# Issuing the key projection between the transposes of later tiles, and loading inputs and first weights ahead of the small vectors, in a one-core encoder step

## The reference, cut to what matters

```python
def rmsnorm(x, g):
    y = xf * lax.rsqrt(jnp.mean(xf * xf, axis=-1, keepdims=True) + NORM_EPS)
    return (y * g).astype(x.dtype)
...
h = rmsnorm(x, norm_mix)
q_sb, k_sb, v_sb, q_sw, k_sw, v_sw, q_mem, gates = split_projection(h, w_in, b_gate)
...
q_sw = rmsnorm(q_sw, q_norm_sw);  k_sw = rmsnorm(k_sw, k_norm_sw)
k, v = jnp.split(rmsnorm(mem, norm_mem) @ w_mem_kv, 2, axis=-1)
```

## Time and profile before

| what | value |
|---|---|
| median of 3 runs | 4260.44 us |
| profiled execution, its time / its span | 4256.27 us / 4254.5 us |
| `project`, from the start to the first matmul of `attend` | 429.74 us |
| in it: until the first projection matmul | 45.04 us |
| start of unit 9, the first of the value block | 112.20 us |
| TensorE busy over the whole span | 83% |

### The profile page before, as it was taken

One profiled execution on the slowest core, in us unless ns is written; L12 is line 12 of the kernel. 1 busy time (PEld: TensorE's weight loads), 2 busy tenths in 40 slices (PEclk: granted clock), 3 DMA queues, 4 the chain that ended last, 5 costly groups with the idle time before them and its releaser, 6 DMA issues.

```text
span 4254.5 us, 35451 instructions
## 1 busy us (share of the span) xinstructions
PE 3514.4 (83%) x10969; PEld 1800.6 (42%) x10969; DVE 2565.3 (60%) x5586; ACT 1509.0 (35%) x3957; POOL 1749.2 (41%) x1439
## 2 busy tenths in 40 slices
PE   7999898889669988768988888996777787777777
PEld 4545665578435454423333344442332333333222
DVE  2131446611878765857866875686775776676444
ACT  2111556611453435343433435443222222233222
POOL 0000000000577677576666666666333333333332
PEclk8999889999889999879999989998999999999999
DMA  5111310044999999999999999999999999999998
GB/s 170 58 41 50 127 45 21 18 158 167 375 397 420 420 421 422 354 401 421 421 421 421 420 411 413 421 407 421 421 418 421 417 413 416 418 416 416 422 422 349
DMA packets 240318, 1402.89 MB, mean 330 GB/s; under 512 B 26096, under 2 KB 54000, under 8 KB 87280
## 3 DMA queue, kind: packets, MB, share of 16 engines
q0 software_dynamic: 165888, 1208.03, 68.8%
q1 hardware_dynamic: 74240, 192.60, 12.2%
HBM read 1368.56 MB, written 32.90 MB: 329 GB/s over the span
## 4 chain that ended last, share of the span: by engine, by line
DMA 22%; POOL 20%; PE 15%; issue 11%; DVE 9%; ACT 2%; POOLq 0%; SPq 0%; ACTq 0%; DVEq 0%
DMA ring<-in_experts_dram,idx 22%; POOL side L1276 11%; POOL ring L1265 9%; PE ps L1386 8%; DVE ring L1643 4%; PE ps L1357 2%; PE ps L1309 2%; PE ps L1334 1%; PE ps L1319 1%; ACT diag L1485 1%; DVE hot L1538 1%; DVE hot L1534 1%; DVE idx L1542 1%; DVE cand L1523 1%; ACT wgt L1476 0%
## 5 line engine op out<-in xcount | busy, mean ns | idle before, releaser
L1386 PE MATMUL ps<-ring,diag 128*128 128x512 f32 x3520 | 1769.1, 647 | 620.2 <-ACT diag L1485 611.4
L1265 POOL DMA_INDIRECT ring<-in_experts_dram,idx x1152 | 1100.6, 955 | 1991.0 <-PE ps L1386 1210.7
L1643 DVE CUSTOM_DVE_ANT_0 ring<-ring,ps 128x1024 f32<-128x1024 f32 x1152 | 1384.8, 1219 | 816.4 <-DMA ring<-in_experts_dram,idx 802.6
L1386 PEld LDWEIGHTS ps<-ring,diag 128*128 128x128 f32 x3520 | 690.6, 204 | 1607.0 <-ACT diag L1485 872.7
L1469 ACT ACTIVATE act_<-hid 128x2 f32<-128x2 f32 x576 | 117.1, 203 | 1916.0 <-DVE hid L1643 1914.8
L1276 POOL TENSOR_TENSOR side<-side,ring 128x1024 f32<-128x1024 f32 x272 | 642.6, 2362 | 57.1 <-ACT ring L1490 51.8
L1309 PE MATMUL ps<-hx,wbuf 128*128 128x256 f32 (+2 forms) x1152 | 397.1, 491 | 13.1 <-DMA hx<-hT_scratch 13.1
L1485 ACT ACTIVATE diag<-const,wgt 128x128 f32<-128x128 f32 x880 | 320.4, 396 | 19.3 <-PE ps L1386 0.5
L1490 ACT ACTIVATE ring<-ring,wgt 128x1024 f32<-128x1024 f32 x272 | 308.2, 1133 | 0.0
L1309 PEld LDWEIGHTS ps<-hx,wbuf 128*128 128x128 f32 x1152 | 223.0, 194 | 178.3 <-issue 110.0
L309 PE MATMUL ps<-w_qkv,hT 128*128 128x512 f32 (+1 forms) x720 | 285.7, 553 | 1.3 <-DVE mhT L403 1.3
(11 more groups left out here) (179 smaller groups left out, 2820.9 us busy)
## 6 DMA issues: line engine op xcount, KB each, us to landing
wbuf<-in_w_gate_o_dram SPq DMA_DIRECT2D x72, 768.0 KB, 8.4
wbuf<-in_w_q_dram SPq DMA_DIRECT2D x24, 1024.0 KB, 9.0
ring<-in_experts_dram,idx POOLq DMA_INDIRECT x1152, 17.1
wbuf<-in_w_out_dram SPq DMA_DIRECT2D x12, 1024.0 KB, 9.0
w_qkv<-in_w_in_dram SPq DMA_DIRECT2D x5, 2048.0 KB, 8.2
o_x<-o_scratch SPq DMA_DIRECT2D x9, 768.0 KB, 30.0
hT_scratch<-hT SPq DMA_DIRECT2D x9, 512.0 KB, 6.7
hx<-hT_scratch SPq DMA_DIRECT2D x9, 512.0 KB, 16.9
```

The costliest lines, as they stand in the source:

```text
L1265: i = nc.gpsimd.indirect_dma_start(out=ring[:, j % RING, :], out_offset=None, in_=A["experts"], in_offset=bass.IndirectOffsetOnAxis(ap=idx ...
L1386: last = nc.tensor.matmul(acc[:, h, :], diag[:, (by_pe(j) - 1) % 4, :], ring[:, j % RING, DM + h * HB:DM + (h + 1) * HB], start=(j % SLOTS ...
L1643: last = nc.vector.tensor_tensor_reduce(out=u, in0=u, in1=xp, scale=1.0, scalar=0.0, op0=ALU.mult, op1=ALU.add, accum_out=hid[:, j % SLOTS ...
```

## The change

Three things are done.

1. **Order on TensorE and ScalarE.** With `BEHIND = 3`, TensorE does for each tile t from 3 on the projection of keys of tile t-3 (`produce`, with `turn(u - 2)` in it) and then the transposes of tile t. Units 0 to 7 stand between transposes, unit 8 and all others behind the last tile. ScalarE evacuates unit t-4 after squaring tile t.
2. **Banks.** As banks 4 to 7 are still in use, all turns of the key block use the one bank 3, and a turn waits for all keeps before it, not for all but one. The squares of the inputs are written into the buffer `mv` rather than PSUM.
3. **Order on SyncE.** Tiles 0 and 1 are loaded right behind the constants, then the two halves of `gmix`, then the weights of the key block, then tiles 2 and 3. The second weights still follow tile 5. The four per-head gain vectors (`gq`, rows spread over 128 partitions) are loaded behind tile 10 and awaited by VectorE only at the first `kvsw` unit.

```diff
         def turn_bank(n):
-            return 3 + n % 2
+            return 3 if n < NT else 3 + n % 2
+        BEHIND = 3
...
                 sp.dma_start(xt[t % XR], TILES[t]).then_inc(x_in[t % XR], 16)
-                if t in (3, 5):
-                    load_w((t - 3) // 2)
+                if t == 1:
+                    ... gmix[:, 0, :] and gmix[:, 1, :] ... .then_inc(gmix_in, 16)
+                if t in (1, 5):
+                    load_w(t // 4)
+            o = 0
+            for name, n in (("q_norm_sw", HD), ("k_norm_sw", HD), ("q_norm_mem", MD), ("k_norm_mem", MD)):
+                sp.dma_start(gq[:, o:o + n], A[name][0:1, :].to_broadcast([P, n])).then_inc(gains_in, 16)
...
-                if n >= 2:
-                    pe.wait_ge(kept, n - 1)
+                if n >= 1:
+                    pe.wait_ge(kept, n if n < NT else n - 1)
...
+            def produce(u):
+                c, kind, t = units[u]
+                if u < NT:
+                    pe.wait_ge(h_done, u + 1)
...
+            for t in range(NX):
+                pe.wait_ge(x_nat, t + 1)
+                if t >= 2:
+                    pe.wait_ge(h_done, t - 1)
+                if t >= BEHIND:
+                    produce(t - BEHIND)
+                for c in range(KC):
+                    last = nc.tensor.transpose(ps[:, 4 + 2 * (t % 2) + c // 4, (c % 4) * P:(c % 4 + 1) * P],
+                                               xt[t % XR][:, c * P:(c + 1) * P], ident)
+                last.then_inc(x_T, 1)
+            pe.wait_ge(h_done, NX)
+            for u in range(NX - BEHIND, len(units)):
+                produce(u)
...
+            for t in range(NX):
+                act.wait_ge(x_in[t % XR], 16 * (t // XR + 1))
...
+                if t > BEHIND:
+                    evacuate(t - BEHIND - 1)
```

More of the change, by code:

```diff
@@ L101, in project @@
         gains_in = sem("gains_in")
+        gmix_in = sem("gmix_in")
         x_in = [sem(f"x_in{i}") for i in range(XR)]
@@ L184, in _ @@
             sp.dma_start(S["const"][:, :], small_dram[:, :]).then_inc(const_in, 16)
[L185 to L191, removed]
             def load_w(c):
@@ L202, in _ @@
                 sp.dma_start(xt[t % XR], TILES[t]).then_inc(x_in[t % XR], 16)
-                if t in (3, 5):
-                    load_w((t - 3) // 2)
+                if t == 1:
+                    with nc.allow_non_contiguous_dma(reason="gains, a few kilobytes"):
+                        sp.dma_start(gmix[:, 0, :], A["norm_mix"][0].rearrange("(c p) -> p c", p=P)).then_inc(gmix_in, 16)
+                        sp.dma_start(gmix[:, 1, :], A["norm_mem"][0].rearrange("(c p) -> p c", p=P)).then_inc(gmix_in, 16)
+                if t in (1, 5):
[3 more added lines that the diff above has]
+                sp.dma_start(gq[:, o:o + n], A[name][0:1, :].to_broadcast([P, n])).then_inc(gains_in, 16)
+                o += n
             for name, c in (("new_swa_k_sample", "cache_swa_k"), ("new_swa_v_sample", "cache_swa_v")):
@@ L266, in _ @@
             pe.wait_ge(const_in, 16)
[L267 to L275, removed]
             def turn(u):
@@ L291, in turn @@
                 last.then_inc(turned, 1)
-            for u, (c, kind, t) in enumerate(units):
+            def produce(u):
+                c, kind, t = units[u]
+                if u < NT:
+                    pe.wait_ge(h_done, u + 1)
                 if t == 0:
@@ L318, in _ @@
         def _(act):
[L319 to L327, removed]
             def keep(u):
@@ L346, in keep, with evacuate @@
                 i.then_inc(kept, 1)
-            for u, (c, kind, t) in enumerate(units):
+            def evacuate(u):
+                c, kind, t = units[u]
                 act.wait_ge(proj, u + 1)
@@ L377, in _ @@
                     keep(u - 2)
+            for t in range(NX):
+                act.wait_ge(x_in[t % XR], 16 * (t // XR + 1))
+                if t >= 1:
+                    act.wait_ge(x_sq, t)
+                nc.scalar.activation(S["mv"][:, :, :].rearrange("p a n -> p (a n)"), xt[t % XR], ACT.Square,
+                                     accum_out=ss[:, 0:1]).then_inc(x_sq, 1)
+                act.wait_ge(x_ms, t + 1)
+                nc.scalar.activation(ss[:, 2:3], ss[:, 1:2], ACT.Sqrt).then_inc(x_rt, 1)
+                if t > BEHIND:
+                    evacuate(t - BEHIND - 1)
+            act.wait_ge(pad_zero, 2)
+            for u in range(NX - BEHIND - 1, len(units)):
+                evacuate(u)
             keep(len(units) - 2)
@@ L382, in _ @@
         def _(dve):
-            dve.wait_ge(gains_in, 16 * 6)
             for t in range(NX + 1):
@@ L395, in _ @@
                     v = t - 1
+                    if v == 0:
+                        dve.wait_ge(gmix_in, 16 * 2)
                     dve.wait_ge(x_T, v + 1)
@@ L408, in _ @@
                 n = n_norm[u]
+                if n == 1:
+                    dve.wait_ge(gains_in, 16 * 4)
                 dve.wait_ge(squared, n)
```

## The result

The changed kernel takes 4272.15 us (median of 14 runs), the kernel before 4258.95 us in the same comparison (14 runs): a ratio of 1.0026, 95% interval 1.0014 to 1.0038. A second comparison gave 4269.93 against 4258.08 us, 1.0030 (1.0017 to 1.0044). By the medians the change costs 12 to 13 us; the intervals reach from 6 to 19 us. The forecast was 4268.2 us, 7.8 us slower, with a range of 4258 to 4275.

A forecast was written before the change was run, and what follows sets the result against it. TensorE was taken to bound the key block from 49.50 us, its head winnable. With both stalls and half clock, unit 9 moved from 112.2 to 120.0 us; that 7.8 us gave 4268.2 us, range 4258 to 4275.

The forecast's parts named there:

- Both pauses: TensorE stalls 5.3 us before turn 2 (unit 3's copy) and some 14.8 us in turn 6 (unit 7's copy).
- The rival that the early outputs pass quickly: Unit 0's output lands by X + 6, so the first stall and its half clock go: 4259.5 us; chance 0.14.
- The strict series: Tile 10, gain vectors, copies and output pass one behind another, unit 0's output landing at X + 15: 4274.4 us; chance 0.13.
- the point (X + 11.7): Landing of unit 0's output from which on the summed slowdown is over 8.5 us, the bound of no change.
- Tile 3 lands at 15.9; with 2.6 us more TensorE reaches its third iteration.: Head of the key block: the third iteration at 18.5, tile 2's transposes done by 18.2 to 19.2; 18.8 taken.
- The sum for the first stall: Unit 3's copy waits for unit 0's output behind tile 10, gains and cache copies: X + 11, bounds X + 6.0 and X + 15.
- I charge 2.2 us for half clock: TensorE loses 2.2 us at the start, bounds 0 and twice that; charged again after the first stall and at unit 9.
- The spill at 280 GB/s: Nine 512 KB DMAs ahead of unit 4's output take 16.9 us; 20.6 us from first issue to that output's landing.
- A microsecond won or lost before unit 9 reaches the end unchanged.: TensorE bounds the stage from 49.50 us on and attend follows, so the 7.8 us at unit 9 were added to the time.
- the condition I had set: The prediction is wrong if the time from unit 9 to the end differs from before by more than 3 us.
- a change within 0.2%: Whole-kernel time within 8.5 us of before, called no change; chance 0.54, against slower 0.38 and faster 0.08.
- The main case: Both stalls as summed, unit 9 7.8 us later, 4268.2 us, own range 4263 to 4272; chance 0.62.

The follow-up runs named there:

- Experiment 1: Changed kernel with the nine spill DMAs and their wait moved behind the first value output; 4250.21 us, ratio 0.9977 against the kernel before.
- experiment 2: Changed kernel with the four gain vectors and two cache copies issued behind the first value output; 4258.31 us, ratio 0.9997 against the kernel before.
- experiment 3: Changed kernel with spill, gain vectors and cache copies all issued later; 4251.14 us, ratio 0.9981 against the kernel before; again 4248.43 us, 0.9980.
- experiment 4: Kernel before with the new order of loads alone, projections still behind all transposes; 4255.75 us, ratio 0.9990 against the kernel before.
- kernel 5: Changed kernel's interleaving alone, with the loads in the order of the kernel before; 4262.61 us, ratio 1.0009 against the kernel before.

## Why the prediction came out right, and where it did not

The terms as predicted and as measured, X being the end of tile 6's transposes:

| step | predicted | measured |
|---|---|---|
| unit 0 starts | 18.8 | 20.54 |
| half clock at its start | 2.2 | 2.2 (unit 0: 20.54 to 29.61, 9.07 for 6.87) |
| X | 52.9 | 54.75 |
| unit 0's output landed, ScalarE goes on | X + 11 | X + 11.9 (66.64) |
| unit 5 starts | X + 14.8 | X + 15.6 (70.39) |
| half clock then | 2.2 | 2.4 (turn and transposes 67.78 to 70.39, 2.61 for 1.30; unit 5 to 78.36, 7.97 for 6.87) |
| last tile multiplied | X + 42.8 | X + 42.7 (97.48) |
| spill to unit 7's copy | 20.6 | 19.15 (97.48 to 116.63) |
| unit 9 starts | 117.8 | 118.67 |
| half clock then | 2.2 | 2.5 (unit 9: 118.67 to 128.09, 9.42 for 6.87) |
| attend, against before | +7.8 | +9.0 |
| time, against before | +7.8 | +13.2 and +11.9 (medians) |

**What was right.** Both pauses, their places, releasers and sizes came from two rules of this program: SyncE issues in its written order, and unit u's copy waits for unit u-3's output to land. Experiment 1 took away the second alone, experiment 2 the first alone, experiment 3 both, each with unit 9 within 2.1 us of what was expected. The rival that the early outputs pass quickly is refuted by 66.64. The strict series, X + 15, did not come either: X + 11.9 is just past the point (X + 11.7) that the prediction named.

**"Tile 3 lands at 15.9; with 2.6 us more TensorE reaches its third iteration."** This failed by 1.7 us. Of these 0.9 are the landing of tile 2, at 15.51 where 1.3 us ahead of 15.9 was expected. The rest is the way behind it. The 2.6 us is the way of a tile that finds the engines free. Here tile 2's landing at 15.51 sets the pace: its scaling (17.31), the multiplication of tile 1 that VectorE's list puts behind it (17.98), and only then tile 3's mean. That is 2.6 + 2.4 us from tile 2, where 2.4 is the cadence that experiment 4 shows from tile to tile.

**The sum for the first stall.** Its terms as printed, 5.7 behind the gain vectors, 2 x 2.1 for the copies and 2.0 for the output, make 11.9, and the prediction wrote 11. The output landed at X + 11.9. With 11.9 the forecast would have been 8.7 us, over the 8.5 that it calls no change. The terms themselves stay in part unconfirmed, since the profile gives no landing of the two cache copies.

**"I charge 2.2 us for half clock"** was near the truth in size at all three places (2.2, 2.4 and 2.5 us lost). But after the first pause 1.3 of the 2.4 fell on turn 2 and tile 7's transposes, which ran in the 2.6 us that the sum already gave to tile 8; the sum was 1.1 us too long there. Nor is the loss a constant: unit 5 took 7.20 us in kernel 1, and the unit behind the long pause 7.87 in kernel 2 and 7.99 in kernel 5, that is 0.3, 1.0 and 1.1 us over the 6.87.

**The spill at 280 GB/s.** The nine transfers took their measured rate again: 289 GB/s at a share of 0.98 in 104.50:118.70, which holds unit 4's output too, and 285 in 99:110 with the spill alone. The Trainium skill's rule of line rate from 512 bytes on ("DMA: Bandwidth & Descriptors", section Specifications) does not hold for this transfer in either kernel. The spill term came out 1.5 us shorter than predicted. A part of that is unit 4's output: it lands 5.6 us behind its issue, not 7.1.

**"A microsecond won or lost before unit 9 reaches the end unchanged."** This step did not hold as written. Up to `attend` the forecast was 1.2 us off. By the medians another 4.2 and 2.4 us arose behind it, where I expected nothing, and the condition I had set (under 3 us from unit 9 to the end) was broken: 4153.3 us in the profile after against 4142.3 before. Of these 11.0 us 2.5 are the half clock at unit 9, 5.1 lie in the attention stage and 3.4 behind it. A single pair of profiles overstates this, because that of before was short and that of after was long, and the medians of the changed kernel aren't clear of the noise (see above). Clear of it is the same step in kernel 3, where 15.5 us up to `attend` gave 9.1.

**The chances.** 0.54 stood on a change within 0.2% and 0.38 on slower; by both medians it is slower, with intervals that begin at 1.0014 and 1.0017. The sum lay 0.7 us inside its bound, while unit 0 (+1.7 us), the first output (+0.9), the half clock behind the first pause (-1.1) and the spill (-1.5) were all off by more and in part made up for each other. That `attend` came out within 1.2 us owes something to luck. The main case had both pauses right, yet the measured 4272.15 lies at the very edge of its own range, 4263 to 4272. Of the 5.4 us between the forecast 7.8 and the measured 13.2, 1.2 arose ahead of `attend` and 4.2 behind it.

## What to carry to other kernels

Work that is brought forward brings its waits with it: before interleaving two stages, list for each buffer that is reused in the earlier stage which DMA must have landed, and what stands ahead of that DMA in its queue. Here an unmoved block of nine DMAs, harmless with 7.6 us of cover, cost a pause of 13 us and ate the whole gain, and issuing it behind the first value output turned +0.26% into -0.23%. Where a gain of 10 us is sought in 4 ms, read it at a stage boundary in the profile, with a repeat, since the stages behind vary by as much.

## What was not expected of the hardware

The attention stage of one and the same kernel took 452.3 us in one execution and 442.1 in another, with a mean granted clock of 0.91 and 0.92.

The clock column says 1.00 for the changed kernel's stretch 20.50:54.80, yet unit 0 took 9.07 us against 6.87 for unit 1 and tile 2's transposes 1.97 us where tile 3's took 1.04. Unit 0's weight loads come every 0.85 us up to 24.1 us and every 0.43 from 24.9 on. So in this trace the column doesn't show what was granted up to there; the durations do. In kernel 1's trace it does read 0.50, in 18.10:20.10.

Four gain vectors of 32 and 64 KB, spread from one row to 128 partitions, cost more queue time than their size: taking them out from ahead of unit 0's output shortened the pause by 2.4 us, 6.17 to 3.81, with X at the same place (54.75 and 54.83), while their 192 KB at the input stream's 393 GB/s would pass in 0.5 us.
